# Hybrid attention block on one core: differential heads' steps put into two gaps of three projection steps

## The chip, the cores and the metric

One NeuronCore of a Trainium2 chip runs the whole program. The metric is the device time of one execution in microseconds, the median of several runs. TensorE is called PE below, VectorE DVE, ScalarE ACT, GpSimd POOL, and SyncE SP, which issues the transfers.

## The reference, cut to what matters

One encoder layer on 1024 tokens of width 1024, all in float32. The input is normalised and multiplied by one combined matrix, which gives queries, keys and values of two head groups:

- group A: 8 query heads on 2 key heads of width 64, a window of two chunks of 64 keys, a sink per head
- group B, "differential attention": 4 heads, each with two query and key sets of width 64 and values of width 128

Group B is what the change touches. For a block of 128 queries it computes

```
s  = q . k / 8 + bias, masked to the chunks up to the query's own     (two sets t = 0, 1)
pr = softmax(s)
a  = pr[0] - lam * pr[1]
o  = a @ v, then a row norm, then the output projection
```

After attention come the output projection, an MLP with a squared relu, a gated add of a second input, and a last norm.

## The kernel before, in words

**Products.** Every large product is made of three float32r passes, high by high, high by low and low by high: each weight and each activation is split into a rounded part (`w_hi`, `u_hi`) and a rest (`w_lo`, `u_lo`). One *projection step* is `half_step` (L1495): for one block of 128 input features, three matmuls of 128 columns of weights with 512 tokens. Eight steps make one job: one 128-wide slice of queries, keys or values for one half of the tokens. `project` (L1521 on) issues steps of a job; at step 0 it waits until POOL has made the rests of the weights (`lo_done`) and until the job's PSUM bank is free (`bank_for`), at step 7 it announces the job (`job_done`).

**Banks.** Jobs, and the turning of values and head outputs ("VT", "AVT", "OT", four transposes by `turn`, L1538), share PSUM banks 6 and 7 in an order fixed by the table `JOBS`. A bank is free when its last result has been copied away, by DVE in `take` (L2082) and `take_o` (L2090), by ACT in `take_turned` (L1065). Head by head the order on bank 6 is: K half 0, VT half 0, Q half 0, OT half 0 (heads 1 and 2), V half 0. For the last head it is AQ0, AVT, AQ2, OT2 half 1, AK.

**Units.** Differential attention is cut into 32 units, 8 query blocks for each of 4 heads, numbered u = 8 hh + k. `ORDER = (0, 7, 1, 6, 2, 5, 3, 4)` gives the query block of k, so that the number of key tiles is 1, 8, 2, 7, 3, 6, 4, 5. Units with odd k have PSUM banks 0 to 3 and the `large` buffers, those with even k banks 4 and 5 and the `small` ones. A unit goes through:

- PE `score_b` (L1606): pairs of 64-row matmuls, six for every 512 keys. It waits until the output of the unit two before has been copied out (`b_oc`)
- DVE `soft_b` (L2106, L2108): bias and negated maximum, for each of the two sets
- ACT `exp_b` (L1072): exponentials with their sums, for each set
- DVE `mix_b` (L2117, L2119, L2123): a = e0 + coef * e1
- PE `trans_b` (L1617): one transpose for each key tile, into the scores' banks. It waits for `b_a`, the end of `mix_b`
- ACT `evac_b` (L1080): copies the transposed tiles to SBUF
- PE `pv_b` (L1629): products with the values. It waits for `b_at`, the end of `evac_b`
- ACT `take_b` (L1089, L1091): scales the output and gives the banks free (`b_oc`)

**Order of the work.** It is written out by hand, one list for each engine, and each engine works through its list in order. Between the pieces of a unit PE works on the projections of the next head, so that ACT and DVE have time for theirs. These steps are numbered by *parts*: a head has 24 parts p of two projection steps each, job p // 4, and unit k has parts 3k, 3k + 1 and 3k + 2. `part_b` (L1711 on) issues the part, and ahead of parts 6, 10, 14 and 18 also a turning: of VT half 0 at part 6 and half 1 at part 10, of OT at 14 and 18 for heads 1 and 2; for the last head AVT at 6, OT2 at 10 and 14. `step_b` of PE (L1730 on) is

```
trans_b(u)  part 3k  pv_b(u)  part 3k+1  score_b(u+2)  part 3k+2
```

In the last two units `score_a(0)` and `score_a(1)` (L1666), the first scores of group A, stand in the place of `score_b`. Behind them comes `step_a(0)`, which begins with `trans_a(0)` (L1679); that waits for `sum_a(0)` on DVE (L2163).

The lists of the other engines, for unit u:

- ACT: evac_b(u), exp_b(u+1) for both sets, take_b(u), and then by k: at k = 2 `take_turned` of VT (or AVT) half 0, at k = 3 of half 1; copies of keys and queries; the rounded weights of a later block (`early_hi`, L1023)
- DVE: soft_b(u+1) for both sets, then at k = 0, 4, 5, 6 a copy of a job or of OT, then mix_b(u+1), then at k = 1, 2, 5, 6 another copy. The copy of OT half 0 (`take_o`; for the last head OT2 half 1) stands at k = 5 between soft_b(u+1) and mix_b(u+1)
- POOL: the rests of weights, keys and queries
- SP: loads of weights, each waiting for its buffer

Of the kernel before, what the change touches and what calls it, by code (L numbers as in the profile page):

```python
# [65 lines left out]
def v_block(h):  # L66

    return 0 if h == 0 else 3 * h


def k_block(h):

    return 1 if h == 0 else 3 * h + 1


def q_block(h):

    return 2 if h == 0 else 3 * h + 2
# [77 lines left out]
def build(nc, x, p, attn_norm_g, w_in, rel_bias, sinks, lam_q1, lam_k1, lam_q2, lam_k2, subln_g, w_out,  # L156
          mlp_norm_g, w_up, w_down, ple_norm_g, w_gate, w_ple, final_norm_g, onehot, out):
    ctx = ExitStack()
    with ctx:
# [127 lines left out]
        def s_at(k, t):  # L287


            return t * T if k % 2 else (4 + t) * HALF  # L290
# [5 lines left out]
        def at_at(k):  # L296

            return at_large if k % 2 else at_small
# [106 lines left out]
        def wait_taken(engine, name, half):  # L405


            engine.wait_ge(job_free[JOB_BANK[name, half]], JOB_TURN[name, half] + 1)
# [1055 lines left out]
        def _(pe):  # L1464
# [22 lines left out]
            def half_step(bank_, s, half, k, xh, xl, first, last):  # L1487

                w0 = s * D + k * P
                wh, wl = w_hi[:, w0:w0 + P], w_lo[:, w0:w0 + P]  # L1490
                x0 = slice(k * T + half * HALF, k * T + (half + 1) * HALF)
                if xh is None:
                    xh, xl, x0 = u_hi[half], u_lo[half], slice(k * HALF, (k + 1) * HALF)
                for n, (w, xx) in enumerate(((wh, xh), (wh, xl), (wl, xh))):
                    mm = nc.tensor.matmul(bank(bank_), w, xx[:, x0], start=(first and n == 0), stop=(last and n == 2))  # L1495
                return mm
# [16 lines left out]
            def bank_for(name, half):  # L1513


                b = JOB_BANK[name, half]
                if JOB_TURN[name, half]:
                    pe.wait_ge(job_free[b], JOB_TURN[name, half])
                return b

            def project(name, half, b, ns, ks=range(DT)):  # L1521


                for n in ns:
                    if n == 0:
                        pe.wait_ge(lo_done, b + 1)
                        bank_for(name, half)
                    mm = half_step(JOB_BANK[name, half], b % 2, half, ks[n], None, None, n == 0, n == DT - 1)
                    if n == DT - 1:
                        mm.then_inc(job_done, 1)  # L1530
# [60 lines left out]
            def score_b(u):  # L1591


                hh, k = u // TT, u % TT
                n = keys_b(k)
                if k < 2:
                    pe.wait_ge(kq_lo, 4 * hh + 3 + k)
                if u >= 2:
                    pe.wait_ge(b_oc, u - 1)
                kh, kl, qh, ql = k_hi[hh], k_lo[hh % 2], q_hi[hh], q_lo[hh % 2]  # L1600
                for c in range(0, n, HALF):
                    w = min(HALF, n - c)
                    for m, (qq, kk) in enumerate(((qh, kh), (ql, kh), (qh, kl))):
                        for t in range(2):
                            rows, s0 = slice(t * HD, (t + 1) * HD), s_at(k, t) + c
                            mm = nc.tensor.matmul(ps[:, s0:s0 + w], qq[rows, ORDER[k] * P:(ORDER[k] + 1) * P],  # L1606
                                                  kk[rows, c:c + w], start=(m == 0), stop=(m == 2))
                            if c + w == n and m == 2:
                                mm.then_inc(b_s, 1)

            def trans_b(u):

                k = u % TT
                pe.wait_ge(b_a, u + 1)
                for n in range(ORDER[k] + 1):
                    o = s_at(k, 0) + n * P
                    mm = nc.tensor.transpose(ps[:, o:o + P], e_at(k, 0)[:, n * P:(n + 1) * P], ident[:, :])  # L1617
                mm.then_inc(b_t, 1)

            def pv_b(u):  # L1620

                hh, k = u // TT, u % TT
                if k == 0:
                    for r in range(2):
                        wait_taken(pe, f"VT{hh}", r)
                pe.wait_ge(b_at, u + 1)
                o = s_at(k, 1)
                for n in range(ORDER[k] + 1):
                    mm = nc.tensor.matmul(ps[:, o:o + P], at_at(k)[:, n * P:(n + 1) * P],  # L1629
                                          v_b[hh % 2][:, n * P:(n + 1) * P], start=(n == 0), stop=(n == ORDER[k]))  # L1630
                mm.then_inc(b_o, 1)

            def turn_v(hh, half):
                wait_taken(pe, f"V{hh}", half)
                turn(f"VT{hh}", half, v_raw)

            def turn_av(half):
                wait_taken(pe, "AV", half)
                turn("AVT", half, v_raw)

            def turn_o(hh, half):
                pe.wait_ge(b_on, hh + 1)
                turn(f"OT{hh}", half, o_b[hh % 2])

            def score_a(v):


                s, i, c0 = v % 2, v // 2, first_key(v)
                half = i // 4
                if v == 0:  # L1650
                    pe.wait_ge(b_oc, N_UNIT - 1)
                elif v == 1:
                    pe.wait_ge(b_at, N_UNIT)
                elif v == 2:
                    pe.wait_ge(b_oc, N_UNIT)
                else:
                    pe.wait_ge(a_lo, v - 2)
                if v in (0, 8):
                    wait_taken(pe, "AK", half)
                if i % 4 == 0:  # L1660
                    for j in range(2 * s, 2 * s + 2):
                        wait_taken(pe, f"AQ{j}", half)
                for jj in range(2):
                    for g in range(2):
                        rows, c = slice(g * HD, (g + 1) * HD), s_a(v) + g * HALF + jj * 256
                        mm = nc.tensor.matmul(ps[:, c + c0:c + 256], aq[2 * s + jj][rows, i * P:(i + 1) * P],  # L1666
                                              ak[rows, (i - 1) * P + c0:(i + 1) * P], start=True, stop=True)
                mm.then_inc(a_s, 1)
# [29 lines left out]
            def job_in(hh, n):  # L1698


                if hh == 3:
                    return ((f"AQ{n}", 0, QA_BLOCK[0] + n) if n < 4 else
                            (("AK", 1, KA_BLOCK[1]), ("AV", 1, VA_BLOCK[1]))[n - 4])
                if n < 4:
                    return ((f"K{hh + 1}", n % 2, k_block(hh + 1)) if n < 2 else
                            (f"Q{hh + 1}", n % 2, q_block(hh + 1)))
                if hh == 2:
                    return (("AK", 0, KA_BLOCK[0]), ("AV", 0, VA_BLOCK[0]))[n - 4]
                return f"V{hh + 2}", n % 2, v_block(hh + 2)

            def part_b(hh, p):  # L1711

                if hh < 3 and p == 6:
                    turn_v(hh + 1, 0)
                if hh < 3 and p == 10:
                    turn_v(hh + 1, 1)
                if hh in (1, 2) and p == 14:
                    turn_o(hh - 1, 0)
                if hh in (1, 2) and p == 18:
                    turn_o(hh - 1, 1)  # L1720
                if hh == 3 and p == 6:
                    turn_av(0)
                if hh == 3 and p == 10:
                    turn_o(2, 0)
                if hh == 3 and p == 14:
                    turn_o(2, 1)
                name, half, b = job_in(hh, p // 4)
                project(name, half, b, range(2 * (p % 4), 2 * (p % 4) + 2))

            def step_b(hh, k):  # L1730

                u = TT * hh + k
                trans_b(u)
                part_b(hh, 3 * k)
                pv_b(u)
                part_b(hh, 3 * k + 1)
                if u + 2 < N_UNIT:
                    score_b(u + 2)
                else:
                    score_a(u + 2 - N_UNIT)  # L1740
                part_b(hh, 3 * k + 2)

            BEHIND = (4, 5, 6, 7, 0, 1, 2, 3)

# [37 lines left out]
            for hh in range(B_HEADS):  # L1782
                for k in range(TT):
                    step_b(hh, k)
# [865 lines left out]
```

## Time and profile before

| what | value |
|---|---|
| median of 3 runs | 1216.71 us (1216.58 to 1216.93) |
| the profiled execution | 1215.57 us |
| its span, from the first to the last instruction | 1213.7 us |
| busy: PE, weight load of PE, DVE, ACT, POOL | 98%, 79%, 59%, 43%, 49% |
| granted clock of PE, mean over the span | 0.996 |
| stretch of the differential heads | about 66 us to 299.5 us |

The profiled execution is 1.1 us below the median. PE's records overlap, since a matmul's end lies behind the start of the next one: a matmul of 512 columns is shown with 389 ns, while the next one starts about 230 ns after it. Durations of PE work are therefore best read from start to start.

### The profile page before, as it was taken

The page shows a single profiled execution, that of the slowest core. Times are in us where ns is not written, and L with a number is a line of the kernel's source. Part 1 is how long each engine was busy: PE and PEld are TensorE (multiplying, and loading weights), DVE is VectorE, ACT ScalarE, POOL GpSimd, SP SyncE. Part 2 cuts the span into 40 slices and gives each one's busy share as a digit, 9 for nine tenths or more (in the row PEclk, how much of TensorE's full clock was granted, in tenths as well). Part 3 has the DMA queues.
Part 4 walks back from the last instruction along what each step waited for, and adds up shares of the span by engine and source line. Part 5 has one row for each costly group of instructions (what it writes and reads, how often), then busy time and mean ns, then how long its engine had stood idle before and what let it go on. Part 6 is the DMA issues. An engine that isn't in the chain of part 4 may idle for free.

```text
span 1213.7 us, 14773 instructions
## 1 busy us (share of the span) xinstructions
PE 1191.8 (98%) x5825; PEld 964.1 (79%) x5825; DVE 710.8 (59%) x927; ACT 518.6 (43%) x858; POOL 600.2 (49%) x284
## 2 busy tenths in 40 slices
PE   6999999999999999999999999999999999999997
PEld 5787787877677788888888888888888888888886
DVE  5245556566767457783937829478294692544233
ACT  6435445455655554423424243243342433442223
POOL 3323222232425567655565556655466555565542
PEclk8999999999999999999999999999999999999999
DMA  6811011123612333425234252342523423121203
GB/s 220 282 36 35 18 36 30 40 53 70 191 36 73 101 125 150 177 70 199 95 122 139 70 183 100 134 139 70 176 102 127 151 70 139 52 78 55 58 1 139
DMA packets 104123, 125.75 MB, mean 104 GB/s; under 512 B 21801, under 2 KB 87382, under 8 KB 98678
## 3 DMA queue, kind: packets, MB, share of 16 engines
q1 hardware_dynamic: 103814, 124.18, 31.2%
q8 instruction: 46, 0.75, 0.3%
q10 hardware_dynamic: 240, 0.62, 0.1%
q14 instruction: 23, 0.19, 0.1%
HBM read 111.14 MB, written 16.01 MB: 105 GB/s over the span
## 4 chain that ended last, share of the span: by engine, by line
PE 94%; DVE 3%; ACT 2%; DMA 1%; SPq 0%; issue 0%; DVEq 0%; ACTq 0%
PE ps L1811 51%; PE ps L1495 23%; PE ps L1471 8%; PE ps L1606 3%; PE ps L1629 3%; PE ps L1617 1%; PE ps L1693 1%; PE ps L1679 1%; PE ps L1666 1%; DMA x_raw<-in_x 1%; ACT e_a L1099 1%; PE ps L1538 1%; PE ps L1554 0%; PE ps L1509 0%; PE ps L1799 0%
## 5 line engine op out<-in xcount | busy, mean ns | idle before, releaser
L883 POOL TENSOR_TENSOR w_lo<-w_raw,w_hi 128x1024 fp32r<-128x1024 f32 x57 | 137.9, 2419 | 148.0 <-ACT w_hi L1008 146.9
L1811 PE MATMUL ps<-block_lo,w_hi 128*128 128x512 f32 x472 | 181.1, 389 | 0.0
L1495 PE MATMUL ps<-u_hi,w_hi 128*128 128x512 f32 x416 | 176.3, 424 | 3.8 <-DVE o_bt L2090 1.7
L752 POOL TENSOR_TENSOR w_lo<-w_raw,w_hi 128x1024 fp32r<-128x1024 f32 x38 | 96.1, 2529 | 163.9 <-ACT w_hi L1023 163.9
L1811 PE MATMUL ps<-up_hi,w_hi 128*128 128x512 f32 x448 | 174.9, 390 | 0.0
L1811 PE MATMUL ps<-up_hi,w_lo 128*128 128x512 f32 x448 | 174.3, 389 | 0.0
L1811 PE MATMUL ps<-up_lo,w_hi 128*128 128x512 f32 x448 | 174.3, 389 | 0.0
L1811 PE MATMUL ps<-block_hi,w_hi 128*128 128x512 f32 x440 | 172.0, 391 | 0.0
L1811 PE MATMUL ps<-block_hi,w_lo 128*128 128x512 f32 x440 | 171.3, 389 | 0.0
L1495 PE MATMUL ps<-u_hi,w_lo 128*128 128x512 f32 x416 | 163.4, 393 | 0.0
L1495 PE MATMUL ps<-u_lo,w_hi 128*128 128x512 f32 x416 | 162.8, 391 | 0.0
L2488 DVE TENSOR_TENSOR h<-ps,h 128x512 f32<-128x512 f32 x224 | 139.2, 677 | 9.5 <-PE ps L1811 9.4
L1008 ACT CAST w_hi<-w_raw 128x1024 fp32r<-128x1024 f32 x56 | 58.8, 1051 | 134.1 <-PE ps L1811 96.7
L1495 PEld LDWEIGHTS ps<-u_hi,w_hi 128*128 128x128 f32 x416 | 78.2, 188 | 32.1 <-issue 17.7
L883 POOL TENSOR_TENSOR w_lo<-raw_x,w_hi 128x1024 fp32r<-128x1024 f32 x29 | 70.3, 2425 | 67.0 <-ACT w_hi L1008 67.0
L1811 PEld LDWEIGHTS ps<-block_lo,w_hi 128*128 128x128 f32 x472 | 88.6, 188 | 18.3
L1811 PEld LDWEIGHTS ps<-block_hi,w_hi 128*128 128x128 f32 x440 | 82.6, 188 | 20.1 <-issue 3.0
L1811 PEld LDWEIGHTS ps<-up_hi,w_hi 128*128 128x128 f32 x448 | 84.1, 188 | 17.8 <-issue 0.4
L883 POOL TENSOR_TENSOR w_lo<-s_sum,w_hi 128x1024 fp32r<-128x1024 f32 x30 | 77.6, 2588 | 41.5 <-ACT w_hi L1008 41.5
L1811 PEld LDWEIGHTS ps<-up_lo,w_hi 128*128 128x128 f32 x448 | 84.1, 188 | 17.6 <-issue 0.2
L1811 PEld LDWEIGHTS ps<-up_hi,w_lo 128*128 128x128 f32 x448 | 84.1, 188 | 17.6
L1811 PEld LDWEIGHTS ps<-block_hi,w_lo 128*128 128x128 f32 x440 | 82.6, 188 | 17.3
(224 smaller groups left out, 2091.8 us busy)
## 6 DMA issues: line engine op xcount, KB each, us to landing
up_lo<-lo_save SPq DMA_DIRECT2D x36, 1024.0 KB, 5.5
w_raw<-in_w_in SPq DMA_DIRECT2D x48, 256.0 KB
w_raw<-in_w_down SPq DMA_DIRECT2D x18, 512.0 KB
w_raw<-in_w_up SPq DMA_DIRECT2D x16, 512.0 KB
raw_x<-in_w_up SPq DMA_DIRECT2D x15, 512.0 KB
raw_x<-in_w_down SPq DMA_DIRECT2D x14, 512.0 KB
x_raw<-in_x SPq DMA_DIRECT2D x8, 512.0 KB, 7.3
h_save<-x_t SPq DMA_DIRECT2D x1, 4096.0 KB, 12.8
```

The costliest lines, as they stand in the source:

```text
L752: nc.gpsimd.tensor_tensor(w_lo[:, s * D:(s + 1) * D], w_raw[:, s * D:(s + 1) * D], w_hi[:, s * D:(s + 1) * D].bitcast(F32), ALU.subtract). ...
L883: nc.gpsimd.tensor_tensor(w_lo[:, s * D:(s + 1) * D], raw, w_hi[:, s * D:(s + 1) * D].bitcast(F32), ALU.subtract).then_inc(lo_done, 1)
L1008: nc.scalar.copy(w_hi[:, s * D:(s + 1) * D], raw).then_inc(hi_done, 1)
L1099: nc.scalar.activation(e_a[s][:, c + c0:c + 256], ps[:, s_a(v) + c + c0:s_a(v) + c + 256], ACT.Exp, bias=nmax_k[:, 4 * s + m:4 * s + m + 1 ...
L1471: mm = nc.tensor.matmul(o[i], w, xx[:, x0[i]], start=(first and n == 0), stop=(last and n == 2))
L1495: mm = nc.tensor.matmul(bank(bank_), w, xx[:, x0], start=(first and n == 0), stop=(last and n == 2))
L1538: mm = nc.tensor.transpose(bank(b)[:, t * P:(t + 1) * P], src[:, c:c + P], ident[:, :])
L1606: mm = nc.tensor.matmul(ps[:, s0:s0 + w], qq[rows, ORDER[k] * P:(ORDER[k] + 1) * P], kk[rows, c:c + w], start=(m == 0), stop=(m == 2))
L1617: mm = nc.tensor.transpose(ps[:, o:o + P], e_at(k, 0)[:, n * P:(n + 1) * P], ident[:, :])
L1629: mm = nc.tensor.matmul(ps[:, o:o + P], at_at(k)[:, n * P:(n + 1) * P], v_b[hh % 2][:, n * P:(n + 1) * P], start=(n == 0), stop=(n == ORDE ...
L1811: mm = nc.tensor.matmul(o, w, xx, start=(first and m == 0), stop=(last and m == 2), skip_group_check=onto)
L2488: nc.vector.tensor_tensor(hq, o, hq, ALU.add).then_inc(dn_free, 1)
```

## The change

It rewrites the order of PE alone. `part_b` gets an argument that picks one or both of a part's two steps, and the turnings move into `part_turns`, called ahead of a part's first step. In `step_b` the middle part is cut in two around `pv_b`, and the third part is moved ahead of the scores. The order for a unit becomes

```
trans_b(u)  part 3k, first step of part 3k+1  pv_b(u)  second step of part 3k+1, part 3k+2  score_b(u+2)
```

so that there are two gaps of three steps instead of three of two, and `score_b(u+2)` stands directly ahead of `trans_b(u+1)`. The number of instructions of every kind is the same, and the lists of ACT, DVE, POOL and SP are not touched.

```diff
-            def part_b(hh, p):
+            def part_b(hh, p, steps=range(2)):
+
+
+                if 0 in steps:
+                    part_turns(hh, p)
+                name, half, b = job_in(hh, p // 4)
+                project(name, half, b, [2 * (p % 4) + i for i in steps])
+
+            def part_turns(hh, p):
 
                 if hh < 3 and p == 6:
                     turn_v(hh + 1, 0)
...
                 if hh == 3 and p == 14:
                     turn_o(2, 1)
-                name, half, b = job_in(hh, p // 4)
-                project(name, half, b, range(2 * (p % 4), 2 * (p % 4) + 2))
 
             def step_b(hh, k):
 
                 u = TT * hh + k
                 trans_b(u)
                 part_b(hh, 3 * k)
+                part_b(hh, 3 * k + 1, range(1))
                 pv_b(u)
-                part_b(hh, 3 * k + 1)
+                part_b(hh, 3 * k + 1, range(1, 2))
+                part_b(hh, 3 * k + 2)
                 if u + 2 < N_UNIT:
                     score_b(u + 2)
                 else:
                     score_a(u + 2 - N_UNIT)
-                part_b(hh, 3 * k + 2)
```

## Rows read from the trace of the kernel before

**Rows 1.** The page: PE's busy time; the chain that ended last, by engine.
```profile
PE 1191.8 (98%) x5825; PEld 964.1 (79%) x5825; DVE 710.8 (59%) x927; ACT 518.6 (43%) x858; POOL 600.2 (49%) x284
...
PE 94%; DVE 3%; ACT 2%; DMA 1%; SPq 0%; issue 0%; DVEq 0%; ACTq 0%
```

**Rows 2.** Waits of PE: total us, times, longest us.
```profile
PE ps L1495 <- DVE o_bt L2090: 1.7, 2, 1.3
...
PE ps L1606 <- ACT o_b L1089: 0.9, 3, 0.5
```

**Rows 3.** Timeline of PE, units 12 and 13: start, us, work, [idle before].
```profile
161.97 0.50 PE L1606 MATMUL ps<-k_hi,q_hi 64*128 64x512 f32 x2
...
162.86 0.66 PE L1538 MATMUL ps<-ident,o_b 128*128 128x128 f32 x4
163.27 0.47 PE L1495 MATMUL ps<-u_hi,w_hi 128*128 128x512 f32 x1
...
164.05 0.40 PE L1495 MATMUL ps<-u_hi,w_hi 128*128 128x512 f32 x1
...
164.74 0.82 PE L1617 MATMUL ps<-ident,e_large 128*128 128x128 f32 x6
165.31 0.48 PE L1495 MATMUL ps<-u_hi,w_hi 128*128 128x512 f32 x1
```

**Rows 4.** Timeline of PE, units 8 and 9.
```profile
126.54 0.50 PE L1606 MATMUL ps<-k_hi,q_hi 64*128 64x512 f32 x2
...
133.06 0.39 PE L1606 MATMUL ps<-k_hi,q_hi 64*128 64x256 f32 x2 [0.18 <-ACT o_b L1089]
...
133.61 0.50 PE L1495 MATMUL ps<-u_hi,w_hi 128*128 128x512 f32 x1
...
134.42 0.39 PE L1495 MATMUL ps<-u_hi,w_hi 128*128 128x512 f32 x1
...
135.10 1.04 PE L1617 MATMUL ps<-ident,e_large 128*128 128x128 f32 x8
```

**Rows 5.** Timelines of ACT and DVE: output of unit 8, mix of unit 9.
```profile
132.65 0.36 ACT L1089 ACTIVATE o_b<-ps,rden 128x128 f32<-128x128 f32 x1
...
133.24 1.29 DVE L2123 SCALAR_TENSOR_TENSOR e_large<-e_large,coef,e_large 128x1024 f32<-128x1024 f32 x1
```

**Rows 6.** Timelines of PE and ACT, unit 10 and the scores of 11.
```profile
140.62 0.50 PE L1606 MATMUL ps<-k_hi,q_hi 64*128 64x512 f32 x2
...
143.75 0.60 PE L1538 MATMUL ps<-ident,v_raw 128*128 128x128 f32 x4
144.11 0.47 PE L1495 MATMUL ps<-u_hi,w_hi 128*128 128x512 f32 x1
...
145.94 0.48 PE L1495 MATMUL ps<-u_hi,w_hi 128*128 128x512 f32 x1
...
145.21 1.01 ACT L1072 ACTIVATE e_large<-ps,nmax 128x896 f32<-128x896 f32 x1
...
146.93 0.57 ACT L1065 COPY v_b<-ps 128x512 f32<-128x512 f32 x1
```

**Rows 7.** Timeline of DVE, unit 13: the copy of OT half 0.
```profile
165.11 0.74 DVE L2090 TENSOR_SCALAR o_bt<-ps,gb 128x512 f32<-128x512 f32 x1
```

**Rows 8.** Timelines of PE and DVE, where group A's steps begin.
```profile
294.75 1.28 PE L1629 MATMUL ps<-v_b,at_large 128*128 128x128 f32 x10
...
299.54 0.66 PE L1679 MATMUL ps<-ident,e_a 128*128 128x128 f32 x4
...
298.80 0.69 DVE L2163 TENSOR_TENSOR e_a<-e_a,rden_a 128x512 f32<-128x512 f32 x1
```

**Rows 9.** PE's idle times of 1 to 2 us, and a stretch's granted clock (PEclk).
```profile
12.14 1.97 PE L1554 MATMUL ps<-ident,x_raw 128*128 128x128 f32 x8 [1.97 <-DMA x_raw<-in_x]
...
332.86 0.47 PE L1495 MATMUL ps<-u_hi,w_hi 128*128 128x512 f32 x1 [1.32 <-DVE o_bt L2090]
...
12.00:15.30 3.30, 2.08 (x9) 1.68 (x10) 2.41 (x3) 2.26 (x4) 0.81 (x2) 0.52 1.05 393
```

## The prediction

> **What bounds the kernel now.** I read the page first. PE is busy for 98% of the span and carries 94% of the chain that ended last; DVE, ACT and DMA have 6% of it together [rows 1]. So time comes and goes with what PE does and with what it must wait for. The list of PE's waits says how little that is: in the stretch of the differential heads three waits for an output copied by ACT, 0.9 us together, one of 0.5 and one of 0.18 among them [rows 2, 4]; the longer of the two waits for OT lies at 332.86, in group A's steps [rows 9]. The 24 parts of each head are thus good cover as they stand. The change adds and removes no instruction. It can act in three ways: by what stands next to what on PE, by the old waits, and by new waits, since every wait of PE's list now meets a differently timed partner. For the last I read ACT's and DVE's timelines beside PE's, and measured everything from the start of a scores block, because the chain of a softmax starts there. All sums are made on the profiled execution, 1215.57 us, which is 1.1 us below the median of 1216.71; the difference is then laid on the median.
>
> **Neighbours on PE.** The third gap vanishes: instead of scores, two steps, transposes there is scores, transposes. The first step behind scores lasts 133.61 to 134.42, 0.81 us, where a step in mid-stream takes 164.05 to 164.74, 0.69: the border costs 0.12 [rows 3, 4]. The border of scores and transposes does not occur for `trans_b`, but four transposes of a turning stand directly behind scores once, 162.86 to 163.27, 0.41 us; behind other transposes the same four take 0.36 [rows 3, 6]. I take their 0.05, the same shapes on the same operands' path, so each unit gains 0.07. The bounds are 0 (a gain of 0.12) and 0.21, the 0.12 of a step behind scores and the 0.09 of a step behind transposes at once (a loss of 0.09). In three units a turning (part 14) used to follow the scores at that same 0.05, so 29 of the 32 gain: 29 x 0.07 = 2.0 us. The turnings of parts 10 and 14 now stand between two steps; a step behind transposes lasts 0.78 instead of 0.69, but the transposes end early by nearly as much: six take 0.57 and four 0.36, so each further one 0.105, by which four would take 0.42 [rows 3, 6]. What is left, 0.03 for each of seven turnings, I count at nothing.
>
> Here the Trainium skill speaks against the change. The page "TensorE: Matmul & The Clock Gate", section "The mechanism", says that a weight load runs ahead of matmuls in flight only where its row group differs; a full-height transpose behind 64-row scores would then wait as a projection step does. By that rule the border would cost what scores and step cost, the 2.0 us would be none, and the result 1229.2. The row with 0.41 against 0.36 says that half or more is saved, and I go by it.
>
> **New wait 1: VT's copy, at k = 2 of all four heads.** Part 8 opens the job Q half 0 (AQ2 in the last head) and needs bank 6, which ACT empties with the copy of VT half 0. In ACT's list that copy is behind both exponentials of unit 11 and the output of unit 10. The second exponential starts 145.21, 4.59 us behind the start of scores 11 at 140.62, and the copy ends at 146.93 + 0.57 = 147.50, which is 6.88 behind it [rows 6]. Nothing in that chain gets shorter, since it is DVE's reductions that release the exponentials. A waiting engine starts 0.05 behind the end it waits for (133.01 to 133.06) [rows 4, 5], so part 8 may start at 6.93. PE before: the first step behind the products starts 145.94, at 5.32, with four steps since the scores [rows 6]. Now three steps lie there, 0.69 less, and 0.07 less for the border: 4.56, and behind one step of 0.78 part 8 is due at 5.34. Before, scores and two more steps stood between, and it was covered. New wait: 6.93 - 5.34 = 1.59, four times: **6.4 us**. Behind it on PE stand part 8, scores 12 and transposes 11; what those feed has enough slack, and unit 11's softmax, shorter than unit 9's (below), is over by then: 6.93 + 1.38 for part 8 is 8.31 even without the scores.
>
> **New wait 2: the long softmax, at k = 1 of heads 1, 2 and 3.** Unit 9 has eight key tiles. From the start of its scores, 126.54, to its transposes, 135.10, PE has 8.56 us with eight steps in it [rows 4]; now six. Its mix ends at 133.24 + 1.29 = 134.53, 7.99 behind [rows 5], a chain of DVE and ACT that PE can't hasten. The scores of unit 10 started at 133.06, at 6.52, released by ACT's copy of unit 8's output, whose place behind both exponentials stays; so they start at 6.52 again, and the old wait of 0.18 grows by the 0.07 that PE comes earlier. They last 0.55 (133.06 to 133.61) [rows 4], and with 0.05 for the border the transposes are due at 7.12, but may start at 8.04: 0.92. Together 0.99 for heads 1 and 2. In head 3 the old wait was 0.5, because ACT rounds a block of weights ahead of its copy there and had to wait for PE's job; that job now ends two steps earlier, against the transposes. I take 0.6 there. Head 0 has eight steps of V1 behind the scores of units 0 and 1, in both orders: none. Sum **2.6 us**. Units with six and five tiles come next; their chains are shorter by some 0.5 us a tile (estimate: a tile's share of 1.29 / 8 in mix, and as much in two reductions and one exponential), against a PE stretch as long as or longer than unit 9's. I count nothing for them; it is one reason for a high end above the forecast.
>
> **New wait 3: OT's copy, at k = 5 of heads 1, 2 and 3.** Part 16 opens a job on bank 6, which DVE empties with the copy of OT behind soft(14). It ends at 165.11 + 0.74 = 165.85, 3.88 behind the start of scores 14 at 161.97 [rows 3, 7], and allows 3.93. On PE part 16 used to be behind the products of unit 13; its first step now stands ahead of them: scores 0.89, border 0.05, six transposes 0.57, two steps 0.78 + 0.69, so due at 2.98 [rows 3]. New wait 0.95, three times: **2.9 us**. Head 0 has no OT; its bank is emptied one unit earlier.
>
> **New wait 4: into group A.** `sum_a(0)` ends at 298.80 + 0.69 = 299.49 and `trans_a(0)` starts at 299.54, the same 0.05 later: it is at its limit already [rows 8]. The chain starts with the products of unit 31 at 294.75, whose output ACT copies ahead of A's exponentials. Four steps lie between; now three, and one border less: 0.69 + 0.07, so **0.75 us** more waiting. Group A's first steps then follow the same chains as before, shifted.
>
> SP and POOL: no load or rest is waited for by PE in this stretch [rows 2], and all come earlier against PE by its waits. Nothing.
>
> **Sum.** 6.4 + 2.6 + 2.9 + 0.75 = 12.6, less 2.0: +10.6 us. Behind 299.5 us PE runs on, busy for 98% as in the whole span [rows 1], so nothing swallows it. Profiled 1226.2; median **1227.3 us**. With the border's bounds (-1.5, +4.6, of which I take three quarters, as that end is far from the nearest row) and a tenth off the waits either way (1.3, not both at once at the top) the forecast's own range is 1224.5 to 1231. A measurement of this kernel tells about 0.2%, 2.4 us, from no change.
>
> **Rivals.**
> - *It gets faster.* Scores and transposes adjacent free ACT of its copy before the exponentials are due, and the longer gaps cover the copies that PE waits for now. If ACT's chain shrank so that VT's copy ended by 5.34 instead of 6.93, and the mix of unit 9 by 7.12, the new waits would be gone: -2.0 and -0.9 for the old waits, 1213.8. Against it: the second exponential follows the reduction, not the copy. Chance 0.03; another 0.03 for a part of it that ends within 0.2%.
> - *The banks are no limit, the softmax alone is.* Waits 1 and 3 missing: 12.6 - 9.3 - 2.0 = +1.3, about 1218; with only wait 1 missing, 1220.9. It would need the copies to come off ACT's and DVE's lists earlier than the written order. Chance 0.06, mostly for the latter.
> - *PE's clock falls in the new waits.* Once an idle of 1.97 us was followed by a granted clock of 0.52 in the next 3.3 us, the level of 1.2 GHz [rows 9]. If each of the four waits of 1.6 us did so for 6.8 us (3.3 at 0.52 and as much again, an estimate), each would cost 3.4 more: +13.6, 1240.9. Against it: an idle of 1.32 us at 332.86 [rows 9], for which PE's records hide 0.2 more, left the clock alone. Chance 0.05. The Trainium skill, same page, section "What's actually happening", lets the clock follow how busy PE has been of late, at half rate when it has been idle. No row shows what gaps of this size do between full stretches.
>
> **How the numbers follow.** Forecast 0.83, the others as given. The range, 1222.5 to 1231, is the forecast's own, 2 us wider at the low end for waits a quarter shorter than summed; the rivals outside it have 0.17. Faster 0.03, same 0.04, slower 0.93.
>
> **What would show it.** The list of PE's waits must show three new releasers: ACT's v_b (and av) copy before a projection, four times some 1.4 us; DVE's e_large before the transposes, three times 0.8; DVE's o_bt, three more times 0.8. The timeline must show scores and transposes adjacent, 0.05 apart from free. If the four waits for v_b are missing, or the transposes behind scores cost over 0.15, the sum is wrong.

## The result, and the profile after

The changed kernel takes 1228.78 us in the median of four runs (1228.18 to 1229.26), the kernel before 1216.64 us beside it (1216.02 to 1216.93): +12.1 us, a ratio of 1.01 with a 95% interval of 1.0083 to 1.0118. The forecast was 1227.3 us.

The page of the changed kernel, busy times and the chain that ended last, to be held against [rows 1]:

```profile
span 1227.4 us, 14773 instructions
...
PE 1192.5 (97%) x5825; PEld 963.9 (79%) x5825; DVE 711.6 (58%) x927; ACT 521.7 (43%) x858; POOL 599.9 (49%) x284
...
PE 91%; DVE 5%; ACT 2%; issue 1%; DMA 0%; POOL 0%; SPq 0%; DVEq 0%; ACTq 0%
```

PE's busy time grew by 0.7 us, the span by 13.7. In the chain PE's share fell from 94% to 91%, and DVE's rose from 3% to 5%. PE did the same work and waited more. For whom, its list of waits says; this is the changed kernel from 65 to 315 us, the stretch of the differential heads (total us, times, longest us):

```profile
PE ps L1495 <- ACT v_b L1065: 4.4, 3, 1.5
PE ps L1617 <- DVE e_large L2130: 2.7, 3, 0.9
PE ps L1495 <- DVE o_bt L2097: 2.7, 3, 0.9
PE ps L1495 <- ACT av L1065: 1.5, 1, 1.5
PE ps L1679 <- DVE e_a L2170: 0.8, 1, 0.8
PE ps L1606 <- ACT o_b L1089: 0.7, 3, 0.2
```

The last line alone was there before [rows 2]. The others are the forecast's four: the copy of VT and AVT (1.5 four times), the mix of the units with eight key tiles (0.9 three times), OT's copy (0.9 three times), the way into group A (0.8 once).

The profiled executions have to be read with one reservation. The first scores start at 66.29 us before and at 67.98 us after:

```profile
67.98 0.33 PE L1606 MATMUL ps<-k_hi,q_hi 64*128 64x128 f32 x2
```

Nothing in the program ahead of that point was changed, and over all kernels of this study it lies between 66.3 and 68.8 us. So I compare the stretch from there to group A's first transposes (299.54 [rows 8], and 313.11 below): 233.26 us before, 245.13 after, **+11.87 us**. What follows takes 914.19 and 914.31 us. The difference of the medians, 12.1, is nearly all in this stretch.

### The profile page after: what moved, and what is told of

It is laid out like the page before. It is cut to its first block, busy times and chain, and to the rows that moved or that the text cites. A ratio compares the mean times of both kernels' runs of the same rounds, so it can differ in the third digit from the quotient of the medians.

```text
span 1227.4 us, 14773 instructions
## 1 busy us (share of the span) xinstructions
PE 1192.5 (97%) x5825; PEld 963.9 (79%) x5825; DVE 711.6 (58%) x927; ACT 521.7 (43%) x858; POOL 599.9 (49%) x284
## 4 chain that ended last, share of the span: by engine, by line
PE 91%; DVE 5%; ACT 2%; issue 1%; DMA 0%; POOL 0%; SPq 0%; DVEq 0%; ACTq 0%
PE ps L1818 50%; PE ps L1495 22%; PE ps L1471 8%; PE ps L1606 3%; PE ps L1629 2%; PE ps L1617 1%; DVE nmax L2115 1%; PE ps L1693 1%; PE ps L1679 1%; PE ps L1666 1%; ACT e_large L1072 1%; DVE ps L2113 1%; ACT e_a L1099 0%; PE ps L1509 0%; PE ps L1806 0%
## 5 line engine op out<-in xcount | busy, mean ns | idle before, releaser
L1495 PE MATMUL ps<-u_hi,w_hi 128*128 128x512 f32 x416 | 174.9, 420 | 12.1 <-ACT v_b L1065 5.0
```

## The waits, one by one

**VT's copy.** PE and ACT of the changed kernel around unit 10 (start, us, work, [idle before]); compare [rows 6]:

```profile
151.06 0.40 PE L1495 MATMUL ps<-u_hi,w_lo 128*128 128x512 f32 x1
152.92 0.48 PE L1495 MATMUL ps<-u_hi,w_hi 128*128 128x512 f32 x1 [1.47 <-ACT v_b L1065]
153.24 0.40 PE L1495 MATMUL ps<-u_lo,w_hi 128*128 128x512 f32 x1
...
150.52 1.01 ACT L1072 ACTIVATE e_large<-ps,nmax 128x896 f32<-128x896 f32 x1 [0.37 <-DVE nmax L2115]
...
151.51 0.36 ACT L1089 ACTIVATE o_b<-ps,rden 128x128 f32<-128x128 f32 x1
...
152.21 0.57 ACT L1065 COPY v_b<-ps 128x512 f32<-128x512 f32 x1
```

Part 8 was due 0.23 behind the matmul at 151.06, at 151.29, and starts at 152.92: 1.63 us. The second exponential waits for DVE's maximum and starts 4.59 us behind the scores of unit 11 (145.93 here), as it did before, and the copy stands behind it and the output. Two small things add up here. The projection step starts 0.14 behind the copy's end (152.78), where I had taken 0.05; and once it has started, its second matmul follows after 0.32 instead of 0.23. So each of these waits costs 1.72 us, not 1.59.

The kernel before shows both, at its one long wait of this kind [rows 9]. OT's copy ended at 332.71, and the projection step started 0.15 later; its second matmul followed after 0.31:

```profile
331.97 0.74 DVE L2090 TENSOR_SCALAR o_bt<-ps,gb 128x512 f32<-128x512 f32 x1
...
332.86 0.47 PE L1495 MATMUL ps<-u_hi,w_hi 128*128 128x512 f32 x1 [1.32 <-DVE o_bt L2090]
333.17 0.40 PE L1495 MATMUL ps<-u_lo,w_hi 128*128 128x512 f32 x1
```

**The mix and the output of unit 9.** PE again, compare [rows 4]:

```profile
137.47 0.39 PE L1606 MATMUL ps<-k_hi,q_hi 64*128 64x256 f32 x2 [0.23 <-ACT o_b L1089]
...
138.99 1.09 PE L1617 MATMUL ps<-ident,e_large 128*128 128x128 f32 x8 [0.90 <-DVE e_large L2130]
```

The scores' wait grew from 0.18 to 0.23, and a wait of 0.90 is new. DVE's mix ends at 138.93, 7.99 behind the start of unit 9's scores at 130.94, exactly as before [rows 5]:

```profile
137.65 1.28 DVE L2130 SCALAR_TENSOR_TENSOR e_large<-e_large,coef,e_large 128x1024 f32<-128x1024 f32 x1
```

**OT's copy.** PE and DVE of the changed kernel, unit 13, compare [rows 7]:

```profile
171.57 0.39 PE L1495 MATMUL ps<-u_hi,w_hi 128*128 128x512 f32 x1
...
173.30 0.47 PE L1495 MATMUL ps<-u_hi,w_hi 128*128 128x512 f32 x1 [0.89 <-DVE o_bt L2097]
...
172.41 0.74 DVE L2097 TENSOR_SCALAR o_bt<-ps,gb 128x512 f32<-128x512 f32 x1
```

Due 0.69 behind 171.57, at 172.26; started at 173.30, again 0.15 behind the copy's end at 173.15. With the late second matmul the wait costs 1.12 us.

**The border** is the extra time of what stands directly behind a block of scores. In the changed kernel that is a group of transposes:

```profile
170.17 0.87 PE L1617 MATMUL ps<-ident,e_large 128*128 128x128 f32 x6
170.79 0.48 PE L1495 MATMUL ps<-u_hi,w_hi 128*128 128x512 f32 x1
```

Six transposes take 0.62 us here; behind a projection step they took 0.57 [rows 3]. The border costs 0.05, as four transposes of a turning had shown. The Trainium skill ("TensorE: Matmul & The Clock Gate", section "The mechanism") lets a weight load run ahead only where row groups differ, by which this border should cost as much as that of scores and step, 0.12. The measurement decides: less than half of it.

**Into group A:**

```profile
313.11 0.66 PE L1679 MATMUL ps<-ident,e_a 128*128 128x128 f32 x4 [0.78 <-DVE e_a L2170]
```

## The experiments

The theory: four kinds of waits, each with its own cause and none in another's way, so that each can be taken away alone and their sum is the loss. The main rival: one common shortage, ACT and DVE as a whole too late for the new order, which shows at these places first and would move to the next ones when they are repaired. Each median below stands beside runs of the kernel before on the same chip; the experiments ran on three chips, so two of them are compared by their difference from the kernel before. "Stretch" is the time from the first scores to group A's first transposes in the profiled execution, against 233.26 us before.

### VT's copy ahead of the exponentials

```diff
                 evac_b(u)
+                if k == 2:
+                    if hh < 3:
+                        take_turned(f"VT{hh + 1}", 0, v_b[(hh + 1) % 2])
+                    else:
+                        take_turned("AVT", 0, av)
                 if u < N_UNIT - 1:
                     exp_b(u + 1, 0)
...
-                if k == 2:
-                    if hh < 3:
-                        take_turned(f"VT{hh + 1}", 0, v_b[(hh + 1) % 2])
-                    else:
-                        take_turned("AVT", 0, av)
```

> The changed kernel, with ACT's copy of VT (AVT) half 0 at k = 2 moved ahead of the two exponentials. After the change that copy ends 6.9 us behind the start of scores 11 and holds part 8 for 1.6 us, and the restart costs a projection step 0.1 more: four times 1.72 us. Theory of separate waits: the copy fits in ACT's idle 0.85 us ahead of the exponentials, the four waits vanish and nothing comes up in their place: 6.9 us less than the changed kernel, about +5.2 us against the kernel before; the waits of transposes on the mix (2.7 us of idle) and on OT's copy stay as they are. Rival, one common shortage: ACT and DVE as a whole are late against the new order of PE, and the bank is only where it shows first; then the time comes back at transposes 11 or later, the list of waits grows elsewhere, and less than half of the 6.9 us is gained (+8.7 us or more against before).

Measured: 1223.00 us, +6.2 against 1216.79; ratio 1.0047 (1.0034 to 1.006). Stretch +6.22. PE's waits from 65 to 315 us:

```profile
PE ps L1617 <- DVE e_large L2130: 2.7, 3, 0.9
PE ps L1495 <- DVE o_bt L2097: 2.6, 3, 0.9
PE ps L1538 <- DVE o_b L2143: 1.0, 1, 1.0
PE ps L1679 <- DVE e_a L2170: 0.8, 1, 0.8
PE ps L1606 <- ACT o_b L1089: 0.7, 3, 0.2
```

All four waits for v_b and av are gone, and those for the mix and for OT's copy stand unchanged. That is the theory's side. But 5.65 us were gained, not 6.9, against the expectation that nothing would come up: PE waits 1.00 us at one new place, the turning of OT2 in the last head, for DVE's norm of the head's output. That could be the rival's shortage, but it isn't: the same norm took 1.22 us in the changed kernel and had ended 2.4 us before PE asked. Here it takes 3.02; why is taken up further down.

### OT's copy a unit earlier

```diff
-                if k == 5 and hh in (1, 2):
-                    take_o(hh - 1, 0)
-                if k == 5 and hh == 3:
-                    take_o(2, 1)
...
                 if u < N_UNIT - 1:
                     mix_b(u + 1)
                 else:
                     sum_a(0)
+                if k == 4 and hh in (1, 2):
+                    take_o(hh - 1, 0)
+                if k == 4 and hh == 3:
+                    take_o(2, 1)
```

> The changed kernel, with DVE's copy of OT half 0 (OT2 half 1 in the last head) moved from k = 5, behind the next softmax's reductions, to the end of k = 4. Theory of separate waits: the turning it copies ends before the mix of k = 4 does, so the copy runs at once and part 16 finds its bank free: three waits of 1.1 us vanish, 3.4 us less than the changed kernel, about +8.7 us against before. Rival of one common shortage: the copy delays the reductions of the next unit, and half or more comes back at transposes or exponentials: +10.4 us or more against before.

Measured: 1225.29 us, +8.5; ratio 1.0067 (1.0054 to 1.008). Stretch +8.40, so 3.47 gained. In PE's waits the three for o_bt are missing, and nothing took their place:

```profile
PE ps L1495 <- ACT v_b L1065: 4.4, 3, 1.5
PE ps L1617 <- DVE e_large L2130: 2.7, 3, 0.9
PE ps L1495 <- ACT av L1065: 1.5, 1, 1.5
```

### The old order at k = 7

```diff
                 trans_b(u)
                 part_b(hh, 3 * k)
-                part_b(hh, 3 * k + 1, range(1))
+                if k < 7:
+                    part_b(hh, 3 * k + 1, range(1))
                 pv_b(u)
-                part_b(hh, 3 * k + 1, range(1, 2))
-                part_b(hh, 3 * k + 2)
+                part_b(hh, 3 * k + 1, range(1, 2) if k < 7 else range(2))
+                if k < 7:
+                    part_b(hh, 3 * k + 2)
                 if u + 2 < N_UNIT:
                     score_b(u + 2)
                 else:
                     score_a(u + 2 - N_UNIT)
+                if k == 7:
+                    part_b(hh, 3 * k + 2)
```

> The changed kernel, with the old order (two steps in each of three gaps) for k = 7 alone, so that eight steps instead of six lie between the scores of the unit with eight key tiles and its transposes, and between the products of unit 31 and group A's first transposes. Theory of separate waits: the waits on the mix (3 x 0.97 us) and on ACT's output copy ahead of scores (3 x 0.29) go, that of group A (0.85) goes too, four borders of scores and step come back at 0.06 each: 4.3 us less than the changed kernel, about +7.8 us against before; in the last head up to 0.4 of a wait on the mix may stay, since ACT rounds a block ahead of it. Waits for VT and OT copies unchanged. Rival: the softmax chains of the units with seven and six key tiles are as tight, and take up what unit 9 gives: 2 us or less gained.

Measured: 1224.35 us, +7.6; ratio 1.0061 (1.0048 to 1.0074). Stretch +7.87, 4.00 gained. Of the mix one wait is left, that of the last head, and the waits for ACT's output and for group A's first transposes are gone:

```profile
PE ps L1495 <- ACT v_b L1065: 4.4, 3, 1.5
PE ps L1495 <- DVE o_bt L2101: 2.6, 3, 0.9
PE ps L1495 <- ACT av L1065: 1.5, 1, 1.5
PE ps L1617 <- DVE e_large L2134: 0.3, 1, 0.3
```

The units with seven and six tiles took nothing up.

### One part of the change: gaps of two and four steps

```diff
                 trans_b(u)
                 part_b(hh, 3 * k)
-                part_b(hh, 3 * k + 1, range(1))
                 pv_b(u)
-                part_b(hh, 3 * k + 1, range(1, 2))
+                part_b(hh, 3 * k + 1)
                 part_b(hh, 3 * k + 2)
```

> One part of the change alone: the third part moves ahead of the scores, but the middle part is not cut, so that the gaps are two steps ahead of the products and four behind them, and scores still stand directly ahead of transposes. Theory of separate waits: VT's waits (6.9 us) and the mix's (2.9) depend on what lies between scores, transposes and part 8, which is the same count as in the change, and stay; OT's (3.4) come from part 16's first step standing ahead of the products and go: about +8.7 us against before. Rival: the cost of the change comes from cutting the middle part (products later, outputs later); then this kernel is within 2 us of the one before.

Measured: 1225.12 us, +8.3; ratio 1.0065 (1.0051 to 1.0079). Stretch +7.79. PE's waits:

```profile
PE ps L1495 <- ACT v_b L1065: 4.4, 3, 1.5
PE ps L1617 <- DVE e_large L2129: 2.7, 3, 0.9
PE ps L1495 <- ACT av L1065: 1.5, 1, 1.5
PE ps L1606 <- ACT o_b L1089: 0.7, 3, 0.2
PE ps L1693 <- ACT at_a L1108: 0.3, 1, 0.3
```

OT's waits are missing, as the theory said, and so is the one into group A, which the expectation left out: with four steps behind the products of unit 31 that chain has its old cover. That makes 4.08 us instead of 3.4. Two thirds of the loss come from moving the scores alone.

### The other part: only the cut around the products

```diff
                 part_b(hh, 3 * k + 1, range(1, 2))
-                part_b(hh, 3 * k + 2)
                 if u + 2 < N_UNIT:
                     score_b(u + 2)
                 else:
                     score_a(u + 2 - N_UNIT)
+                part_b(hh, 3 * k + 2)
```

> The other part of the change alone: the middle part is cut around the products, so that gaps are three steps, one step, and two steps behind the scores, which stay in their old place. Theory of separate waits: the mix's and the VT copy's waits come from scores standing directly ahead of transposes, so none of them is here; part 16's first step stands ahead of the products, but with two more steps since the scores it is due at 4.4 us against the OT copy's 4.0, so that wait is missing as well; the waits of scores for ACT's output copy stay near the old 0.9 us in all, since the step count between scores is the same, with a single step of cover between products and scores for the short ones. Within 0.5 us of the kernel before. Rival: products later make outputs later, one step (0.7 us) does not cover ACT's 0.4 us copy with its queue, and scores wait 0.3 us or more in many of the 32 units: +3 us or more.

Measured: 1217.63 us against 1217.15; ratio 1.0002 (0.9992 to 1.0012), no difference that can be told. PE waits 1.0 us ahead of scores for ACT's output, where it was 0.9, and there is one new wait:

```profile
PE ps L1606 <- ACT o_b L1089: 1.0, 3, 0.7
PE ps L1679 <- DVE e_a L2170: 0.6, 1, 0.6
```

The stretch of its profiled execution is 1.13 us longer than before, twice the 0.5 expected. The larger part, 0.69, is the way into group A, which this expectation left out as well: from the products of unit 31 to group A's first transposes PE takes 4.79 us in all three kernels (298.24 to 303.03 here, 294.75 to 299.54 before, 308.32 to 313.11 in the changed one), and the cut puts one more step ahead of those products. The other 0.44 grows by hundredths from unit to unit. The parts do not add up to the change: +7.8 for the one, +1.1 for the other, +11.87 together. The missing 3 us are in the main OT's waits, 3.4 us, which need both: scores without the steps behind them, and part 16 ahead of the products.

### The three repairs together

The edits are the three above, of VT's copy, of OT's copy and of k = 7.

> The three repairs together on the changed kernel: ACT's VT copy ahead of the exponentials, DVE's OT copy a unit earlier, the old order at k = 7. Theory of separate waits: from the first scores of the differential heads to group A's first transposes the three single runs took 5.65, 3.47 and 4.00 us off the changed kernel's +11.87; summed they leave -1.25, and with the old waits ahead of scores gone too the kernel is 1 to 2.5 us faster than the one before: PE's list of waits in that stretch shows only 0.3 us for a mix and up to 1.0 us for a head norm (o_b). Rival, the waits share their causes: repairs overlap, and 2 us or more of waits come up at other places, so that it ends at or above the kernel before.

Measured: 1215.33 us against 1216.76; ratio 0.9991 (0.9983 to 1.0), just at the edge of what can be told. Stretch -1.33 against before: 13.20 us off the changed kernel, and the three alone had taken 5.65 + 3.47 + 4.00 = 13.12. They add up, the 1.00 us of the head norm included:

```profile
PE ps L1538 <- DVE o_b L2147: 1.0, 1, 1.0
PE ps L1617 <- DVE e_large L2134: 0.3, 1, 0.3
```

### The copies moved in the kernel before

> The kernel before, PE's order untouched, with the VT and the OT copy moved as in the two repairs. Theory of separate waits: in the old order both banks are free long before PE asks (part 8 begins 0.7 us or more behind the end of the VT copy), so moving the copies is worth nothing: within 0.3 us of the kernel before. Rival: the repairs are gains in themselves (ACT and DVE less late in general), and the kernel before gets faster by 1 us or more, too.

The edits are the first two, on the kernel before. Measured: 1217.12 us against 1216.76; ratio 1.0004 (0.9995 to 1.0013); stretch -0.05. The copies were worth nothing while the old order covered them; what they cost in the changed kernel comes from the cover that the change took away.

### Why the head norm was late

In the VT repair, DVE and POOL in the last head (start, us, work), and PE behind them:

```profile
268.96 3.02 DVE L2143 TENSOR_TENSOR o_b<-o_b,rs_b 128x1024 f32<-128x1024 f32 x1
...
268.51 2.39 POOL L752 TENSOR_TENSOR w_lo<-w_raw,w_hi 128x1024 fp32r<-128x1024 f32 x1 [5.14 <-ACT w_hi L1023]
...
272.04 0.66 PE L1538 MATMUL ps<-ident,o_b 128*128 128x128 f32 x4 [1.00 <-DVE o_b L2143]
```

The same instruction took 1.22 us there in the kernel before and in the changed one, where it began 0.26 and 0.03 us ahead of POOL's subtraction. Here POOL's subtraction was under way when it began. The VT repair did that itself: AVT's copy no longer stands ahead of ACT's rounding of block 17, so ACT rounds, and POOL subtracts, half a microsecond sooner against DVE's norm. The changed kernel:

```profile
274.43 1.22 DVE L2143 TENSOR_TENSOR o_b<-o_b,rs_b 128x1024 f32<-128x1024 f32 x1
...
274.46 3.42 POOL L752 TENSOR_TENSOR w_lo<-w_raw,w_hi 128x1024 fp32r<-128x1024 f32 x1 [5.62 <-ACT w_hi L1023]
```

The edit lets ACT round block 17 a unit later, so that POOL subtracts it later:

```diff
-                elif k in (1, 2, 4, 5, 6):
-                    early_hi(16 + (1, 2, 4, 5, 6).index(k))
+                elif k in (1, 3, 4, 5, 6):
+                    early_hi(16 + (1, 3, 4, 5, 6).index(k))
```

> The VT repair plus one move: in the last head ACT rounds weight block 17 at k = 3 instead of k = 2, so that POOL's subtraction of that block (2.4 us) no longer runs beside DVE's head norm. In the VT repair alone that norm took 3.02 us instead of the 1.22 of the kernel before, and PE waited 1.00 us for it ahead of OT2's turning. Theory, the two engines slow each other down: the norm is back at 1.2 to 1.3 us, PE's wait for o_b (1.00) is gone, and the time is 1.0 us below the VT repair. Rival, the norm is long for another reason (its operands, its place in DVE's list): it stays near 3 us and so does the wait.

Measured: 1222.89 us, +6.1 against 1216.76; ratio 1.005 (1.0036 to 1.0064). The VT repair alone had +6.2: no gain that can be told in the medians, where 1.0 us was expected. The trace shows the mechanism and what took half of the gain:

```profile
267.85 1.22 DVE L2143 TENSOR_TENSOR o_b<-o_b,rs_b 128x1024 f32<-128x1024 f32 x1
...
274.50 2.37 POOL L752 TENSOR_TENSOR w_lo<-w_raw,w_hi 128x1024 fp32r<-128x1024 f32 x1 [12.24 <-ACT w_hi L1023]
...
276.93 0.50 PE L1495 MATMUL ps<-u_hi,w_hi 128*128 128x512 f32 x1 [0.47 <-POOL w_lo L752]
```

The norm is back at 1.22 us and the wait for it is gone, but the block is now late itself, for 0.47 us. Stretch +5.72, 0.50 less than with the VT repair alone.

### All of it, and the better place for block 17

The three repairs, and block 17 rounded at the end of k = 3:

> All three repairs with the move of block 17's rounding. Theory of separate waits: as the three together, minus whatever wait for the head norm is left there (0 to 1.0 us): 2 to 3 us faster than the kernel before, waits of PE in the stretch of the differential heads 0.3 us or less. Rival: at or above the kernel before, since DVE meets POOL elsewhere.

Measured: 1215.23 us against 1216.76; ratio 0.9988 (0.9978 to 0.9997). Stretch -1.78, short of the 2 us expected by the 0.47 of the late block. The next kernel rounds the block behind `evac_b` of k = 3 instead of at that unit's end:

```diff
                 evac_b(u)
+                if (hh, k) == (3, 3):
+                    early_hi(17)
...
-                elif k in (1, 3, 4, 5, 6):
-                    early_hi(16 + (1, 3, 4, 5, 6).index(k))
+                elif k in (1, 4, 5, 6):
+                    early_hi(16 + (1, 2, 4, 5, 6).index(k))
```

> The three repairs, with block 17 rounded at k = 3 of the last head directly behind the copy of the transposes instead of at the end of the unit. In the variant that rounds it at the end of k = 3, the head norm was short (1.22 us) but PE waited 0.47 us for the block. Theory of separate waits: rounding it 4 us sooner ends that wait, the norm stays at 1.22 us since POOL's 2.4 us start behind it, and the stretch from first scores to group A's first transposes is 0.5 to 0.6 us below that variant's 231.48 us, 2.3 us below the kernel before; only 0.3 us of wait for a mix is left. Rival: the rounding, now ahead of two exponentials, makes a wait of its own, 0.5 us or more, at transposes or scores.

Measured: 1214.84 us against 1217.15; ratio **0.9977** (0.9966 to 0.9987). Stretch -2.52, 0.74 less than with block 17 at the unit's end, where 0.5 to 0.6 were expected. It is the best kernel of the study, 0.2% faster than the one before. One wait is left in its differential heads:

```profile
PE ps L1619 <- DVE e_large L2136: 0.3, 1, 0.3
```

## Why the prediction was right, point by point

| term of the forecast | forecast, us | measured, us | how |
|---|---|---|---|
| VT's copy, four times | 6.4 | 6.9 | 1.72 each in the timeline; 5.65 + the 1.00 that came up in its run |
| mix and output, heads 1 to 3 | 2.6 | 2.7 | start to start 0.97 at the transposes, three times; the scores' three waits 0.2 less in all, since that of 0.51 in head 3 shrank to 0.23 |
| OT's copy, three times | 2.9 | 3.4 | 1.12 each; 3.47 in its run |
| into group A | 0.75 | 0.85 | 1.50 from A's scores to the transposes, 0.65 of it the scores |
| borders, 29 units | -2.0 | about -2.0 | the remainder of the stretch; 0.07 a unit by the transposes' 0.05 above |
| sum | +10.6 | +11.87 | stretch of the profiled execution |

The signs named in the forecast came as written: three new releasers, four, three and three times, and the transposes 0.05 dearer behind scores. The waits were not luck, then: each was found where it was forecast, and taken away alone. The term that was mis-sized is the price of a wait itself. "A waiting engine starts 0.05 behind the end it waits for" was read from scores that waited for ACT; a projection step that waits for a copy out of its bank starts 0.14 to 0.15 behind, and its second matmul then comes 0.07 to 0.09 late. That is 0.13 for each of VT's four waits and 0.17 for each of OT's three, 1.0 us of the 1.3 that were missing. The wait at 332.86 in the kernel before had shown both. It is not a property of every projection step: the one that waited for POOL at 276.93 above started 0.06 behind the end of POOL's subtraction (274.50 + 2.37 = 276.87), though spans on POOL are rough. Why the two differ stays open.

The rivals. *It gets faster*: no; the mix still ends at its old distance, 7.99 us, behind the scores, and the second exponential still waits for DVE. *The softmax alone is the limit*: no; the two copies that empty bank 6 cost 10.3 of the table's 13.8 us of waits. *PE's clock falls*: no; the mean granted clock is 0.996 as before, and the page's row of the granted clock in 40 slices of the changed kernel has its one low slice at the start:

```profile
PEclk8999999999999999999999999999999999999999
```

None of the four idle times of 1.47 us cost clock: the granted clock is 1.00 from 66 to 320 us. The idle time of 1.97 us that was followed by the half clock [rows 9] lies in the start, where PE had its first instruction at 5.71 us and worked until 10.17. Behind the first scores no run here has an idle time of PE over 1.5 us, so none shows what a longer one would cost.

The sum without a gain at the borders, 1229.2 us, lies nearer to the measured 1228.78 than the forecast does, but by luck: the borders gave their 2 us, and the waits cost 1.2 us more than summed.

## What to carry to other kernels

A hand-written order gives each wait a cover, counted in steps between the instruction that sets off a chain and the one that needs its end; when steps are moved, list for each chain the steps between before and after, the copies that free a shared bank as much as the softmax. Neighbours on PE were worth 0.07 us a unit here, lost cover 0.85 to 1.7 us wherever it fell short. And where a new order is short of cover at a few places, look at the other engines' lists: two copies moved to earlier places in ACT's and DVE's lists took back 9.1 of 11.9 us, and with the old order at one unit in eight and one block's rounding moved, a loss of 1% became a gain of 0.2%.

## What the runs showed of the hardware that was not expected

DVE's head norm, 128 x 1024 by two operands in SBUF, takes 1.22 us alone, and 3.02 us when it begins 0.45 us behind a subtraction of POOL of 2.39 us: it ends 1.08 us behind POOL's end, so it did next to nothing meanwhile. In the kernel before, at the same place, it was DVE that came first, and then POOL's subtraction was the long one (3.20 instead of 2.39; 3.42 in the changed kernel); moving POOL's away brought the norm back to 1.22. The Trainium skill, page "SBUF — State Buffer", section "Who interferes with whom", tells of an exclusive lock on a port pair that the two share, says that a DVE instruction with two SBUF inputs contends with a GpSimd instruction that reads SBUF, and that the order of issue decides who blocks; these traces agree with it, from both sides.

Two profiled executions, of the cut alone and of the VT repair with block 17 moved, each the slowest run of its kernel, took 917.0 us from group A's first transposes to the end, where the others took 914.2 to 914.7, with three waits of 0.3 to 1.2 us of PE for DVE in the MLP. Their programs are the same there, so the change doesn't explain it, and the cause stays open.
